# Layer two's expert rows: one gather of 64 whole rows into 64 partitions, or of 128 half rows into all 128

## The reference, cut to what matters

```python
def _ec_moe(h, router, w_gate, w_up, w_down):
    B, n, _ = h.shape
    cap = CAPACITY_FACTOR * n // N_EXPERTS          # 2 * 512 // 16 = 64
    aff = jax.nn.softmax((h @ router).astype(jnp.float32), axis=-1)
    g, idx = lax.top_k(jnp.swapaxes(aff, 1, 2), cap)
    xs = h[bidx, idx]                               # 64 rows of 1024 for each expert
    a = jnp.einsum('becd,edf->becf', xs, w_gate)    # 1024 x 1024 weights, three per expert
    u = jnp.einsum('becd,edf->becf', xs, w_up)
    y = jnp.einsum('becf,efd->becd', jax.nn.silu(a) * u, w_down) * g[..., None]
    return jnp.zeros_like(h).at[bidx, idx].add(y)
```

## Time and profile before

| | |
|---|---|
| median of three runs | 1862.16 us (1861.97 to 1863.17) |
| profiled execution, span from first to last instruction | 1860.3 us; no time beside its span was recorded for it |
| TensorE busy / weight loads busy | 1761.5 us (95%) / 897.9 us (48%) |
| VectorE / ScalarE / GpSimd busy | 798.5 / 357.2 / 228.8 us |
| HBM read | 506.94 MB |
| hardware DMA queue q1 (SP's loads) | 66672 packets, 478.66 MB, 64.0% of 16 engines |
| software DMA queue q0 (POOL's transfers) | 14128 packets, 44.84 MB, 7.8% |
| DMA, last 10 of 40 slices | 9 tenths or more in nine of them, 400 to 413 GB/s |

### The profile page before, as it was taken

The page is one execution under the profiler, slowest core; times in us unless marked ns, Lnnn a source line. Parts: engine busy times, 40 slices in busy tenths (PEclk is TensorE's granted clock), DMA queues, the critical chain, the costliest instruction groups (busy, mean ns, idle before and its releaser), DMA issues.

```text
span 1860.3 us, 30895 instructions
## 1 busy us (share of the span) xinstructions
PE 1761.5 (95%) x13218; PEld 897.9 (48%) x13218; DVE 798.5 (43%) x1624; ACT 357.2 (19%) x776; POOL 228.8 (12%) x313
## 2 busy tenths in 40 slices
PE   7999999999999999999998999999989999888896
PEld 4886567744444444443433886577433333222222
DVE  3995667678511111111112684776242333223232
ACT  3313455622100000000001313565210000000001
POOL 1000341011112121111211001410010000000000
PEclk9999999999999999999999999999999999999999
DMA  9544000086799999999998833001869999999996
GB/s 398 232 153 161 1 1 2 1 351 256 264 401 392 394 397 391 397 391 392 396 397 299 342 153 136 1 24 47 343 255 400 404 403 405 413 407 408 411 411 273
DMA packets 83137, 525.68 MB, mean 283 GB/s; under 512 B 11280, under 2 KB 13600, under 8 KB 24128
## 3 DMA queue, kind: packets, MB, share of 16 engines
q1 hardware_dynamic: 66672, 478.66, 64.0%
q0 software_dynamic: 14128, 44.84, 7.8%
q10 hardware_dynamic: 2208, 0.26, 0.1%
HBM read 506.94 MB, written 16.79 MB: 282 GB/s over the span
## 4 chain that ended last, share of the span: by engine, by line
PE 64%; DMA 22%; DVE 8%; ACT 3%; issue 3%; SPq 1%; POOL 0%; POOLq 0%; DVEq 0%; ACTq 0%
PE psum L1645 14%; PE psum L1639 9%; DMA arena<-in_w_up 8%; PE psum L1648 7%; PE psum L1315 6%; DMA ring<-in_w_up 6%; PE psum L1511 5%; PE psum L1397 5%; PE psum L1273 3%; PE psum L1442 3%; PE psum L1415 2%; PE psum L1371 2%; ACT arena L1096 2%; DMA arena<-in_w_down 2%; DMA ring<-in_w_down 2%
## 5 line engine op out<-in xcount | busy, mean ns | idle before, releaser
L1645 PE MATMUL psum<-ring,arena 128*32 128x512 f32 x1856 | 242.2, 593 | 1.9 <-DMA ring<-in_w_down 1.6
L1639 PE MATMUL psum<-ring,arena 128*64 128x512 f32 x888 | 206.6, 600 | 19.0 <-DMA ring<-in_w_down 12.4
L1182 ACT ACTIVATE arena<-psum 128x768 f32<-128x768 f32 (+1 forms) x32 | 22.5, 704 | 899.0 <-PE psum L1648 466.6
L1639 PE MATMUL psum<-arena 128*64 128x512 f32 x648 | 151.2, 600 | 13.7 <-DMA arena<-in_w_up 7.7
L1511 PE MATMUL psum<-ring,arena 128*128 128x512 f32 x320 | 143.5, 598 | 0.8 <-DVE arena L2032 0.8
L1648 PE MATMUL psum<-ring,arena 128*32 128x256 f32 x1856 | 142.6, 379 | 0.0
L1096 ACT ACTIVATE arena<-psum,smx 128x768 f32<-128x768 f32 (+4 forms) x160 | 119.0, 749 | 95.8 <-DVE smx L2003 95.8
L1639 PEld LDWEIGHTS psum<-ring,arena 128*64 128x64 f32 x888 | 58.3, 136 | 150.8 <-issue 109.2
L2003 DVE TENSOR_REDUCE smx<-psum 128x1 f32<-128x768 f32 (+4 forms) x160 | 115.8, 765 | 29.6 <-PE psum L1355 22.7
L1648 PEld LDWEIGHTS psum<-ring,arena 128*32 128x32 f32 x1856 | 60.3, 110 | 138.8 <-issue 138.8
L1645 PE MATMUL psum<-arena 128*32 128x512 f32 x960 | 125.2, 593 | 0.8 <-DMA arena<-in_w_down 0.8
(11 more groups left out here) (319 smaller groups left out, 2060.0 us busy)
## 6 DMA issues: line engine op xcount, KB each, us to landing
ring<-in_w_down SPq DMA_DIRECT2D x85, 1024.0 KB, 29.4
ring<-in_w_up SPq DMA_DIRECT2D x80, 1024.0 KB, 29.1
ring<-in_w_gate SPq DMA_DIRECT2D x78, 1024.0 KB, 28.9
arena<-in_w_gate SPq DMA_DIRECT2D x50, 1024.0 KB, 29.4
arena<-in_w_up SPq DMA_DIRECT2D x48, 1024.0 KB, 28.6
arena<-in_w_down SPq DMA_DIRECT2D x43, 1024.0 KB, 29.0
ring<-in_w_adat SPq DMA_DIRECT2D x32, 1024.0 KB, 6.4
ring<-in_w_in SPq DMA_DIRECT2D x18, 1024.0 KB, 20.7
```

Of the source, the lines that this page charges most:

```text
L1639: ins = mm(psum[64 * n:64 * n + 64, b * 512:(b + 1) * 512], lhs(k), w[:, n * 512:(n + 1) * 512], start=k == 0, stop=k == KD - 1)
L1645: ins = mm(psum[r0:r0 + 32, b * 512:(b + 1) * 512], lhs(k)[:, 32 * g:32 * g + 32], w[:, n * 512:(n + 1) * 512], start=k == 0, stop=k == KD ...
```

## The change

In layer two `xg` has 512 columns instead of 1024, and `gidx` has 128 partitions. Half-row numbers from `jT` replace `iT` for the last layer: the DMA gathers 128 half rows of 2 KB, the first halves of the 64 rows into partitions 0 to 63 and the second halves into 64 to 127. Four transposes of 128 x 128 turn them. Each result then holds, in its columns 0 to 63, features of the first half, and in columns 64 to 127 features of the second; VectorE's scaling reads them in that order and writes `xs` as before. `iT` is no longer made in the last layer, and `jT` raises `ri` instead. Layer one keeps its code.

```diff
-    xg = [area(BIG + 10240, D), area(MOE1 + 1536, D)]
+    xg = [area(BIG + 10240, D), area(MOE1 + 1536, 512)]
...
-    gidx = sb("gidx", [CAP, 1], U32)
+    gidx = sb("gidx", [P, 1], U32)
...
                 pool.wait_ge(*L("ri", 1))
-                plink(pool, pool.tensor_copy(gidx[0:CAPX, :], iT[0:CAPX, 0:1]))
...
+            half_rows = xnd.rearrange("t (h n) -> (t h) n", h=2)
+
+            def row_numbers(e):
+
+                return jT[:, 0, e] if l == DEPTH - 1 else iT[0:n_tok, e]
+
             def gather():
+                if l == DEPTH - 1:
+                    pool.indirect_dma_start(out=xg[l], out_offset=None, in_=half_rows,
+                                            in_offset=bass.IndirectOffsetOnAxis(ap=gidx[:, 0:1], axis=0)
+                                            ).then_inc(L["gat"], 16)
+                    return
...
             else:
+                plink(pool, pool.tensor_copy(gidx[:], row_numbers(slice(0, 1))))
                 gather()
+            n_idx = P if l == DEPTH - 1 else n_tok
             pool.wait_ge(*L("gat", 16))
             pool.wait_ge(*L("xt", 1))
-            plink(pool, pool.tensor_copy(gidx[0:n_tok, :], iT[0:n_tok, 1:2]))
+            plink(pool, pool.tensor_copy(gidx[0:n_idx, :], row_numbers(slice(1, 2))))
             gather()
...
-                    pool.tensor_copy(gidx[0:n_tok, :], iT[0:n_tok, bass.ds(e + 2, 1)]).then_inc(L["gi"], 1)
+                    pool.tensor_copy(gidx[:], row_numbers(bass.ds(e + 2, 1))).then_inc(L["gi"], 1)
...
-                rows, step = (CAPX, CAPX) if last else (CAP, P)
-                for k in range(KD):
-                    ins = tr(bank(0, rows, k * step), xg[l][0:rows, k * P:(k + 1) * P], ident[0:rows, 0:rows])
+                if last:
+                    for j in range(4):
+                        ins = tr(bank(0, P, j * P), xg[l][:, j * P:(j + 1) * P], ident[:])
+                else:
+                    for k in range(KD):
+                        ins = tr(bank(0, CAP, k * P), xg[l][0:CAP, k * P:(k + 1) * P], ident[0:CAP, 0:CAP])
                 ins.then_inc(L["xt"], 1)
...
-                dve.tensor_copy(iT[0:CAPX, :], token[0:CAPX, :]).then_inc(L["ri"], 1)
-                ts(jT[:, 0, :], token[:], spread[:, 0:1], spread[:, 1:2], ALU.mult, ALU.add)
+                if last:
+                    ts(jT[:, 0, :], token[:], spread[:, 0:1], spread[:, 1:2], ALU.mult, ALU.add).then_inc(L["ri"], 1)
+                else:
+                    dve.tensor_copy(iT[0:CAPX, :], token[0:CAPX, :]).then_inc(L["ri"], 1)
+                    ts(jT[:, 0, :], token[:], spread[:, 0:1], spread[:, 1:2], ALU.mult, ALU.add)
...
-            turned = psum[:, 0:512 if last else 1024].rearrange("p (k m) -> p k m", k=8)
+            turned = psum[:, 0:1024].rearrange("p (k m) -> p k m", k=8)
+            turned_halves = psum[:, 0:512].rearrange("p (j h m) -> p h j m", j=4, h=2)
+
+            def by_half(ap):
+
+                return ap.rearrange("p (h j) m -> p h j m", h=2)
...
-                for s, a, b in parts:
+                if last:
+                    ins = tt(by_half(xs[l][par]), turned_halves,
+                             by_half(acol[:, l, 1, :, 0:1]).broadcast_to([P, 2, 4, CAPX]), ALU.mult)
+                for s, a, b in [] if last else parts:
```

## The result

The changed kernel takes 1847.78 us (median of 4 runs, 1846.37 to 1848.39), the kernel before 1862.07 us beside it (4 runs). The ratio is 0.9924, with a 95% interval of 0.991 to 0.9938: 14.3 us faster, or 11.5 to 16.8 with the interval.

A forecast was written before the change was run, and what follows sets the result against it. The prediction took the end of layer two's weight stream as the bound. Gathers -11.8, later signal +0.11 and transposes -0.05 summed to -11.7 us, so 1862.2 became 1850.5 us, range 1848 to 1860.

The forecast's parts named there:

- What bounds the kernel: Layer two's experts: the end of the never-pausing weight stream sets the time; TensorE's speed inside an expert is worth nothing.
- The cause named, the uneven partitions: Layer two's gathers load lower partitions more, slowing packets 0.9 us each; spreading removes this, chance 0.68, 1849 to 1854 us.
- the first term of the sum: Layer two's 14 gathers in the weight stream fall from 1.54 to 0.70 us each, gaining 11.8 us.
- The mean of seven windows of 18 us: Old gather's cost to the weight stream, from seven gathers between 1536 and 1779: 1.54 us.
- The floor of the range: Whole kernel's fastest expected time: 1862.2 - 12.7 + 0.1 = 1849.6 us, less 1 us; range starts at 1848.
- 1 us if losses of 1.71 are typical: Allowance taken off the fastest expected time if layer two's old gathers typically cost 1.71 us: 1 us.
- The start, +0.06 us: Start of layer two's experts: later routing signal costs 0.11 us, four transposes instead of eight save 0.05 us.
- the gather is hidden with 1.3 us to spare: Start of layer two: TensorE's filler matmuls end at 1381.8, after the gather lands at 1380.5 at most.
- the 1384.1 forecast: Layer two's first expert matmul was to start at 1384.1 us, a sign that the prediction is right.
- VectorE's new order: VectorE's scaling of the turned rows: same elements in another order, costed at 0, bounds 0 and +0.7 us at the start.
- POOL's issue in the loop: POOL's gather issue in layer two's expert loop may grow from 1.32 to 1.6 to 2.1 us, costing nothing.
- The rule on descriptors: Layer two's gather: small transfers are descriptor-dominated and the change doubles descriptors, so by that rule alone it would cost more.

The follow-up runs named there:

- e1: Kernel before with layer two's same 64 whole rows gathered into partitions 32 to 95 instead of 0 to 63; 1848.37 us, ratio 0.9933.
- e6: Kernel before without layer two's 14 gathers of experts 2 to 15, so part of the computation is left out; 1838.71 us.
- e7: Changed kernel without layer two's 14 gathers of experts 2 to 15, so part of the computation is left out; 1837.12 us.
- e2: Kernel before with layer two's 64 whole rows gathered into partitions 64 to 127; 1862.45 us, ratio 1.0006.
- e3: Kernel before with layer two's gather split into two DMAs of 64 half rows, both into partitions 0 to 63; 1861.65 us, ratio 1.0002.
- e9: Kernel before with layer two's 64 whole rows gathered into partitions 16 to 79, 48 in the lower half and 16 in the upper; 1860.88 us.
- e0: Kernel before run once more, unchanged, to look at its start of the stage; 1861.76 us, ratio 0.9999.

## Why the prediction was right, and where it was wrong

- What bounds the kernel, and that more of a gather's price is slowness than bytes: right, and shown by e1, e6 and e7. The cause named, the uneven partitions, is right in e1, e2, e3; e9 shows that the excess isn't in proportion to "the lower partitions more than the upper ones". What inside the chip the rows share isn't shown.
- **The step that failed is the first term of the sum, 14 x (1.54 - 0.70) = 11.8 us, mis-sized.** It measured 14 x (1.69 - 0.66) = 14.4 us. The old gather costs 1.69 us and not 1.54, which is 2.1 of the 2.6 us; the new one 0.66 and not 0.70. The mean of seven windows of 18 us was too low for two reasons. I took the clean rate from one window of 14 us, 0.4193 MB/us; over 250 us of e6 the weights moved at 105.11 / 250 = 0.4204, and with that the same seven windows give 1.59 us. And all seven lay after 1536, while the earlier gathers cost more. The queue of the weights from 1400 to 1540, first before and then e6:

```profile
q1 hardware_dynamic: 7583, 55.23, 97.9%
```

```profile
q1 hardware_dynamic: 8090, 58.88, 101.1%
```

These 3.65 MB are 8.7 us for five gathers and the end of a sixth, up to 1.74 us each; from 1550 to 1800 it is 99.73 against 105.11 MB, 12.8 us for eight gathers, 1.60 each. Why the earlier ones cost more is open. The earlier trace rows had hinted at it, with 405 GB/s in the first stretch against 409 in the second.
- The floor of the range stood on the same 1.54 us, 12.7 us of gain at most, and took off "1 us if losses of 1.71 are typical". That step is wrong by its own numbers: 14 x (1.71 - 0.63) = 15.1 us is 2.4 us more, and the floor would have been 1847 us.
- The start, +0.06 us: the signal did come later, and four transposes saved 0.05 us. But "the gather is hidden with 1.3 us to spare" was read from an execution at the low clock and with a landing of 3.8 us "at most", which was the median of two gathers; this one took 4.0. At the full clock there is no cover in the kernel before. The first expert matmul began at 1382.58 and not at the 1384.1 forecast, since this execution had the full clock. The change is worth 0.5 us there, by one trace of the changed kernel, and 0.2 us or less at the low clock.
- VectorE's new order took 0.69 us as before: right. POOL's issue in the loop took 1.40 us and not 1.6 to 2.1; hidden, as said.
- The rule on descriptors was no rule against the change. The Trainium skill ("DMA: Bandwidth & Descriptors", section "Bandwidth") calls transfers under 64 KB descriptor-dominated. A gather has 256 KB in either kernel, and the 128 pieces of 2 KB went in the 80 packets of 64 pieces of 4 KB.

## What to carry to other kernels

When the DMA engines are full, look at GB/s at a full share as well as at the share: a stretch that is full at a lower rate holds a transfer that slows the others. In this kernel a gather into 64 partitions of one half (or into 16 to 79) beside a full stream cost more than its bytes, 1.5 to 1.7 us for 0.62 us of bytes, though it is small and nobody waits for it. Spread such rows evenly over both halves: 32 to 95 did, and so did half rows over all 128. And price a transfer from the length of the whole stream, not from a few short windows.

## What the runs showed of the hardware that was not expected

- The excess isn't in proportion to the difference of the halves: 48 + 16 rows cost (442.4 - 420.9) / 14 = 1.54 us a gather, 64 + 0 cost 1.69 (1.60 in e2, with the rows in the upper half), 32 + 32 cost 0.66.
- 128 indirect pieces of 2 KB made as many packets of rows as 64 pieces of 4 KB, 64 of 4 KB each, whether in one DMA over 128 partitions or in two over 64; at the old place they cost the stream the same (444.7 and 444.5 us).
- The granted clock after the routing was at the lower of its two levels for some microseconds in five of the eleven traces, with either start (0.50 of full speed, that is 1.2 GHz, in the microseconds from 1378 to 1380 of before), and the stage then starts about 1.0 us later before and 1.5 us later after the change. From 1373 to 1376 TensorE was busy for 0.6 us in before (clock low afterwards), and for 1.2 us in e0 and 1.0 us in the changed kernel (full clock), so what decides it is open.
